# Key and query remainders spread over idle stretches and units, finer waits in three small stages, and the values of four attention blocks in one run

## The reference

```python
for layer in range(DEPTH):                                 # first block
    x = x + 0.5 * swiglu_ffn(x, ffn1_norm[layer], ...)
    if layer % 2 == 0:
        x = x + retention_dilated_mixer(x, ...)
    else:
        x = x + stick_breaking_mixer(x, ...)
    x = x + 0.5 * swiglu_ffn(x, ffn2_norm[layer], ...)
x = rms_norm(x, final_norm)
...
y_pool = pool_mixer(u, pool_w, pool_scale)                 # second block, each layer
y_nsa = nsa_mixer(q, kv[:, :, 0], kv[:, :, 1], gates, q_norm, k_norm, cmp_pe, cmp_w1, cmp_w2)
mix = jnp.concatenate([y_pool, y_nsa], axis=-1) @ w_out
x = x + gate1 * mix
h2 = rms_norm_2(x, norm2) * (1.0 + scale2) + shift2
return x + gate2 * (jnp.square(jax.nn.relu(h2 @ w_ff1)) @ w_ff2)
```

## Time and profile before

| | us |
|---|---|
| median of three runs (lowest, highest) | 3198.38 (3194.66, 3199.76) |
| the profiled execution | 3204.74 |
| its span, first to last instruction | 3203.0 |
| PE busy | 3175.9 |
| DVE busy | 1728.2 |
| POOL busy | 1303.5 |
| ACT busy | 1149.8 |
| mean granted clock of PE | 0.996 |

### The profile page before, as it was taken

How to read it: one execution, slowest core, us unless ns; L and a number is a source line. 1 busy time by engine, 2 the same in 40 slices (tenths; PEclk the granted TensorE clock), 3 DMA queues, 4 the chain that set the end, 5 groups by cost and what they waited for, 6 DMA issues and landing times.

```text
span 3203.0 us, 40631 instructions
## 1 busy us (share of the span) xinstructions
PE 3175.9 (99%) x15480; PEld 2549.3 (80%) x15480; DVE 1728.2 (54%) x2194; ACT 1149.8 (36%) x1700; POOL 1303.5 (41%) x688
## 2 busy tenths in 40 slices
PE   9999999999999999999999999999999999999999
PEld 7888886788888888887678888876888888678887
DVE  5544546554445444446764444776645556765443
ACT  4223312532223222236752222457322343753222
POOL 4777201067672777400016765030557402115600
PEclk9999999999999999999999999989999999999999
DMA  7554331155443554331124443410434342034432
GB/s 220 147 154 148 130 110 60 54 153 148 144 153 116 144 151 157 119 96 49 53 80 137 145 150 119 95 63 28 150 131 145 118 101 90 27 99 138 131 101 82
DMA packets 338612, 371.48 MB, mean 116 GB/s; under 512 B 32704, under 2 KB 287808, under 8 KB 338240
## 3 DMA queue, kind: packets, MB, share of 16 engines
q1 hardware_dynamic: 311040, 277.99, 28.1%
q0 software_dynamic: 27456, 91.94, 9.2%
HBM read 361.92 MB, written 2.18 MB: 114 GB/s over the span
## 4 chain that ended last, share of the span: by engine, by line
PE 46%; DVE 2%; ACT 2%; issue 0%; DVEq 0%; ACTq 0%
PE ps L394 19%; PE ps L779 16%; PE ps L471 2%; PE ps L685 1%; PE ps L1109 1%; PE ps L1121 1%; PE ps L1435 1%; PE ps L625 1%; PE ps L1948 1%; PE ps L566 0%; PE ps L990 0%; PE ps L1887 0%; DVE w_lo L342 0%; DVE sb_scr_lo L1412 0%; PE ps L705 0%
## 5 line engine op out<-in xcount | busy, mean ns | idle before, releaser
L338 ACT CAST w_hi<-raw 128x2048 fp32r<-128x2048 f32 x243 | 463.8, 1909 | 1139.0 <-PE ps L394 925.0
L394 PE MATMUL ps<-h_hi,w_hi 128*128 128x512 f32 x2064 | 807.3, 391 | 1.7 <-DVE w_lo L342 1.2
L394 PE MATMUL ps<-h_hi,w_lo 128*128 128x512 f32 x2064 | 804.2, 390 | 0.0
L394 PE MATMUL ps<-h_lo,w_hi 128*128 128x512 f32 x2064 | 804.1, 390 | 0.0
L342 DVE TENSOR_TENSOR w_lo<-raw,w_hi 128x2048 fp32r<-128x2048 f32 x241 | 608.5, 2525 | 248.9 <-ACT w_hi L338 248.6
L779 PE MATMUL ps<-a_hi,w_hi 128*128 128x512 f32 x1325 | 516.6, 390 | 0.4
L779 PE MATMUL ps<-a_lo,w_hi 128*128 128x512 f32 x1325 | 515.6, 389 | 0.0
L779 PE MATMUL ps<-a_hi,w_lo 128*128 128x512 f32 x1325 | 515.5, 389 | 0.0
L394 PEld LDWEIGHTS ps<-h_hi,w_hi 128*128 128x128 f32 x2064 | 388.1, 188 | 82.2 <-DVE w_lo L342 1.7
L394 PEld LDWEIGHTS ps<-h_hi,w_lo 128*128 128x128 f32 x2064 | 388.1, 188 | 81.2
L394 PEld LDWEIGHTS ps<-h_lo,w_hi 128*128 128x128 f32 x2064 | 388.2, 188 | 79.8 <-issue 0.2
(11 more groups left out here) (385 smaller groups left out, 4115.3 us busy)
## 6 DMA issues: line engine op xcount, KB each, us to landing
raw<-in_ffn_w_in SPq DMA_DIRECT2D x174, 512.0 KB, 5.0
raw<-in_w_ff SPq DMA_DIRECT2D x128, 512.0 KB, 4.3
m_in<-in_w_mod POOLq DMA_DIRECT2D x96, 512.0 KB, 4.1
raw<-in_ffn_w_out SPq DMA_DIRECT2D x88, 512.0 KB, 4.2
m_in<-in_w_ff POOLq DMA_DIRECT2D x64, 512.0 KB, 4.0
raw<-in_hyb_w_in SPq DMA_DIRECT2D x28, 512.0 KB, 4.5
raw<-in_w_in SPq DMA_DIRECT2D x28, 512.0 KB, 4.7
raw<-in_sb_w_in SPq DMA_DIRECT2D x24, 512.0 KB, 4.1
```

What stands on the lines that cost most here:

```text
L338: eng.copy(w_hi[:, e % 2], raw[:, e % 2]).then_inc(s["w_hi_done"], 1)
L394: mm = pe.matmul(ps[:, bank], wbuf[a][:, e % 2, at:at + P], hbuf[b][:, k], start=(k == 0 and n == 0), stop=(k == KC - 1 and n == 2))
```

## The change

- **Retention:** the two turns of six DVE operations are halved; three operations each stand in units 8, 9, 13 and 14.
- **Group norm:** the first mean matmul waits for three copies, the second for four, where both waited for four.
- **Stick-breaking:** chunks 4, 5 and 7 of the output projection go to banks 2, 3 and 2 instead of 7; chunks 4 and 5 wait for an exponential that was read from their bank instead of for the last eviction.
- **NSA operands:** highs and lows get orders of their own. Highs and lows of key group 0 move to steps of the key and query norm before (`nsa_pre`); the lows of queries 2 and 3 stand ahead of the compressed branch's chain, 4 and 5 behind it, 6 and 7 in units 18 and 19; the high of query 7 in unit 16. Some operands lie in other buffers.
- **Fill:** shares of a group's four units are (0, 5, 5, 6) in NSA instead of (4, 4, 4, 4), and (6, 14, 14, 14) in the dilated loop instead of (12, 12, 12, 12).
- **Values:** in the dilated loop, and in NSA from group 2 on, the values of a group's four units are done in one run in the next group's first iteration.

```diff
@@ -690,6 +690,9 @@
 
+        def om_bank(d):
+            return {4: 2, 5: 3, 7: 2}.get(d, 7)
+
@@ -697,12 +700,14 @@
             for d in range(KC):
-                if d:
-                    pe.wait_ge(s["om_x"], d)
+                if d in (4, 5):
+                    pe.wait_ge(s["sb_exp"], 2 * c.sb + 28)
+                elif d:
+                    pe.wait_ge(s["om_x"], d if d < 6 else d - 2)
...
-                        mm = pe.matmul(ps[:, 7], wbuf[a][:, c.slab % 2, at:at + P], om_part(k, b),
+                        mm = pe.matmul(ps[:, om_bank(d)], wbuf[a][:, c.slab % 2, at:at + P], om_part(k, b),
@@ -734,8 +739,17 @@
 
-            lo, per = spec["fill"]
-            return lo + (12 * d + 11) // per
+            return next(i for i in range(4 * len(spec["pairs"])) if filled(spec, i + 1) >= 12 * (d + 1))
+
+        def fill_share(spec, i):
+            return spec["fill"][i % 4] if i >= spec["from"] else 0
+
+        def filled(spec, upto):
+            return sum(fill_share(spec, i) for i in range(upto))
+
+        def in_one_run(spec, i):
+
+            return i // 4 >= spec["runs"]
@@ -951,10 +965,13 @@
 
-        def dve_turn(eng, c, xs, cos, sin, tmp, moved=m_two):
-            c.moved += 2
-            eng.wait_ge(s["rope_moved"], 32 * c.moved)
+        def dve_turn(eng, c, xs, cos, sin, tmp, moved=m_two, half=None):
+            if half != 1:
+                c.moved += 2
+                eng.wait_ge(s["rope_moved"], 32 * c.moved)
             for i, (x, _) in enumerate(xs):
+                if half is not None and i != half:
+                    continue
@@ -1078,15 +1095,27 @@
             n = 4 * len(spec["pairs"])
-            lo, per = spec["fill"]
             fill = pe_out_half(pe, c)
+
+            def values(j):
+                hp, br, I = att_unit(spec, j)
+                a, ag = c.att + j, c.attg + j // 4
+                pe.wait_ge(s["att_pt"], 2 * (a + 1))
+                if I == 3:
+                    pe.wait_ge(s["att_rc"], ag)
+                for o in range(2):
+                    mm = pe.matmul(ps[qk_rows(o), o_bank(ag), I * P:], spec["v"](br, 2 * hp + o, I),
+                                   p_T(a, o)[:, 4 * I * P:(3 * I + 4) * P], start=(I == 3), stop=(I == 0),
+                                   skip_group_check=True)
+                mm.then_inc(s["att_o"], 1)
+
...
-                if lo <= i < n:
-                    advance(fill, per)
+                if 0 <= i < n:
+                    advance(fill, fill_share(spec, i))
@@ -1099,17 +1128,11 @@
                     pe_outp_ahead(pe, c)
-                if i >= 1:
-                    hp, br, I = att_unit(spec, i - 1)
-                    a, ag = c.att + i - 1, c.attg + (i - 1) // 4
-                    pe.wait_ge(s["att_pt"], 2 * (a + 1))
-                    if I == 3:
-                        pe.wait_ge(s["att_rc"], ag)
-                    for o in range(2):
-                        mm = pe.matmul(ps[qk_rows(o), o_bank(ag), I * P:], spec["v"](br, 2 * hp + o, I),
-                                       p_T(a, o)[:, 4 * I * P:(3 * I + 4) * P], start=(I == 3), stop=(I == 0),
-                                       skip_group_check=True)
-                    mm.then_inc(s["att_o"], 1)
+                if i >= 1 and not in_one_run(spec, i - 1):
+                    values(i - 1)
+                elif i >= 1 and i % 4 == 0:
+                    for j in range(i - 4, i):
+                        values(j)
@@ -1146,7 +1169,7 @@
                     a = c.att + i
-                    eng.wait_ge(s["att_o"], a)
+                    eng.wait_ge(s["att_o"], c.att + i // 4 * 4 if in_one_run(spec, i) else a)
@@ -1376,31 +1399,38 @@
         dil_spec = {
-            "pairs": [(hp, 0) for hp in range(4)], "y": 16, "mask": "mask_dil", "gate": None, "layer": None, "fill": (8, 12), "parts": 2,
+            "pairs": [(hp, 0) for hp in range(4)], "y": 16, "mask": "mask_dil", "gate": None, "layer": None, "fill": (6, 14, 14, 14), "from": 8, "runs": 0, "parts": 2,
...
-            "pairs": [(hp, br) for hp in range(4) for br in range(2)], "y": 4, "mask": "mask_causal", "layer": 0, "fill": (7, 4), "parts": 4,
+            "pairs": [(hp, br) for hp in range(4) for br in range(2)], "y": 4, "mask": "mask_causal", "layer": 0, "fill": (0, 5, 5, 6), "from": 7, "runs": 2, "parts": 4,
...
-        QK_ORDER = (("k", 0, 0), ("q", 0), ("q", 1), ("k", 0, 1), ("q", 2), ("q", 3), ("q", 4), ("q", 5), ("q", 6),
+        HI_ORDER = (("k", 0, 0), ("k", 0, 1), ("q", 0), ("q", 1), ("q", 2), ("q", 3), ("q", 4), ("q", 5), ("q", 6),
                     ("k", 1, 0), ("k", 1, 1), ("q", 7))
-
-        def qk_count(upto):
-            return sum(2 if item[0] == "k" else 1 for item in QK_ORDER[:QK_ORDER.index(upto) + 1])
+        LO_ORDER = (("k", 0, 0), ("k", 0, 1), ("q", 0), ("q", 1), ("q", 2), ("q", 3), ("q", 4), ("q", 5),
+                    ("k", 1, 0), ("k", 1, 1), ("q", 6), ("q", 7))
+
+        def qk_count(order, upto):
+            return sum(2 if item[0] == "k" else 1 for item in order[:order.index(upto) + 1])
...
-            in_act, at = ((1, 16), (1, 19), (0, 2), (0, 3), (0, 6), (0, 7), (0, 1), (1, 14))[h]
-            return act_r[:, at] if in_act else sb_scr_lo[:, at * SEQ:(at + 1) * SEQ]
+            in_act, at = ((1, 0), (1, 1), (1, 2), (1, 3), (0, 6), (0, 7), (0, 1), (1, 14))[h]
+            return act_r[:, at] if in_act else scr_r(at)
+
+        def scr_r(at):
+            return sb_scr_lo[:, at * SEQ:(at + 1) * SEQ]
...
-            return act_r[:, (((0, 1), (2, 3)), ((12, 17), (13, 18)))[g][br][low]]
+            if (g, low) == (0, 1):
+                return scr_r(2 + br)
+            return act_r[:, ((16, 12), (19, 13), (None, 17), (None, 18))[br + 2 * low][g]]
...
@@ -1427,9 +1457,9 @@
             pe.wait_ge(s["att_max"], 2 * (c.att + i))
-            if i in (0, 4, 8, 16, 24):
-                upto = {0: ("q", 1), 4: ("k", 0, 1), 8: ("q", 3), 16: ("k", 1, 1), 24: ("q", 7)}[i]
-                pe.wait_ge(s["qk_lo"], 16 * l + qk_count(upto))
+            if i in (0, 8, 16, 24):
+                upto = {0: ("q", 1), 8: ("q", 3), 16: ("k", 1, 1), 24: ("q", 7)}[i]
+                pe.wait_ge(s["qk_lo"], 16 * l + qk_count(LO_ORDER, upto))
@@ -1710,8 +1740,8 @@
                     if step == 0:
-                        pe.wait_ge(s["ret_copy"], 4)
                         for g in (0, 1):
+                            pe.wait_ge(s["ret_copy"], 3 + g)
@@ -2242,13 +2272,11 @@
                         eng.activation(p, p, ACT.Exp, scale=HD ** -0.5).then_inc(s["cb_exp"], 1)
-                    for h in range(2, 7):
+                    for h in range(4, 7):
...
-                        eng.wait_ge(s["qk_lo"], 16 * l + qk_count(("q", 1 + 2 * br)))
+                        eng.wait_ge(s["qk_lo"], 16 * l + qk_count(LO_ORDER, ("q", 1 + 2 * br)))
                         act_k_high(eng, 1, br)
-                    eng.wait_ge(s["qk_lo"], 16 * l + qk_count(("q", 5)))
-                    act_q_high(eng, 7)
@@ -2269,6 +2297,9 @@
                             part_hi(eng, c.slab + 1, i - 8, 4)
+                        elif i == 16:
+                            eng.wait_ge(s["qk_lo"], 16 * l + qk_count(LO_ORDER, ("q", 5)))
+                            act_q_high(eng, 7)
@@ -2287,6 +2318,10 @@
                         act_hn_root(eng, c, P, 16)
+                        eng.wait_ge(s["rope_done"], 16 + 7 * l + 2)
+                        eng.wait_ge(s["cm_kp"], 2 * (l + 1))
+                        for br in range(2):
+                            act_k_high(eng, 0, br)
@@ -2307,10 +2342,8 @@
                                      k_cmp[g * HD:(g + 1) * HD, 0, 0:N_CMP]).then_inc(s["kd_copy"], 1)
-                        act_k_high(eng, 0, 0)
-                        act_q_high(eng, 0)
-                        act_q_high(eng, 1)
-                        act_k_high(eng, 0, 1)
+                        for h in range(4):
+                            act_q_high(eng, h)
@@ -2703,9 +2736,9 @@
                             gn_copy(pair - 1)
-                        if i in (8, 13):
+                        if i in (8, 9, 13, 14):
                             eng.wait_ge(s["evac_dve"], c.proj)
-                            dve_turn(eng, c, slab_rope(c, 0 if i == 8 else 1), "cos_dil", "sin_dil", nbuf)
+                            dve_turn(eng, c, slab_rope(c, i // 13), "cos_dil", "sin_dil", nbuf, half=(i - 8) % 5)
@@ -2839,7 +2872,7 @@
                             eng.wait_ge(s["om_mm"], d + 1)
-                        eng.scalar_tensor_tensor(xT[:, d], ps[:, 7], 1.0, xT[:, d], ALU.mult, ALU.add
+                        eng.scalar_tensor_tensor(xT[:, d], ps[:, om_bank(d)], 1.0, xT[:, d], ALU.mult, ALU.add
@@ -2902,7 +2935,8 @@
 
-                    dve_k_low(eng, l, 0, 1)
+                    dve_q_low(eng, l, 2)
+                    dve_q_low(eng, l, 3)
@@ -2933,8 +2967,8 @@
                                       ALU.mult).then_inc(s["cb_w"], 1)
```

(15 more changed lines are left out.)

## The result

| | before | after |
|---|---|---|
| median of seven runs (lowest, highest), us | 3198.38 (3194.66, 3203.01) | 3209.95 (3206.89, 3212.38) |
| the profiled execution, us | 3204.74 | 3206.89 |
| its span, us | 3203.0 | 3205.1 |
| TensorE busy, us | 3175.9 | 3164.1 |
| mean granted clock | 0.996 | 0.998 |

The ratio is 1.0031, with a 95% interval of 1.0021 to 1.0041: slower by some 10 us. The forecast was 3202 with a range of 3184 to 3212; the time lies in the range, but beyond the 0.2% that the forecast called no change. A few executions of the kernels took from 3636 to 12593 us instead of some 3200, and the ratios leave them out.

What follows compares the result with a forecast made beforehand. TensorE, busy 3175.9 of 3203.0 us, was taken as the bound, so only its gaps and small stream losses could be won. Gains 21.4 less losses 25.2 made 3.8 us slower than the median 3198.38: 3202, range 3184 to 3212.

Steps and rivals of the forecast that it cites:

- Small stages: Retention, group norm and stick-breaking: shorter TensorE waits gain 0.9, 0.9 and 1.6 us.
- Start of NSA: Both NSA layers: TensorE gaps ahead of L1887 go, 6.5 us; layer 0's clock no longer falls, 2.2 (bounds 0 and 2.9).
- a difference of a few us carries over unscaled: Whole kernel: sums made on the profiled 3204.74 us apply to the median 3198.38, 0.2% below.
- Moved work: NSA remainders and casts moved into VectorE and ScalarE gaps: nothing lost; L1004 0.5 us late in layer 1, with slack.
- Values in a run, NSA, and reciprocals: NSA units: skips gain 7.0 and copy waits 1.7 us; reciprocals lose 13.5 and 0.9, exponentials 2.4 and 1.6.
- The waits for reciprocals: NSA units 12, 16, 20, 24, 28, two layers: TensorE stalls 1.35 us at L1095, together 13.5.
- The waits for exponentials: Filled NSA groups: TensorE arrives 0.2 us early in each of 12, 2.4 lost; layer ends lose 1.6.
- The price of a skip: NSA: each skipped switch from scores to values and back saves about 0.19 us, 36 times: 7.0.
- The four waits for evictions: Dilated units 11, 12, 14, 15: chunks wait for their bank's eviction, 0.9, 2.3, 1.1 and 2.2 us.
- for reciprocals at units 4 and 8: Dilated stage: waits for reciprocals at these units lose 0.3 us, part of the 6.8.
- 0.6 gained: Dilated loop: 12 skipped switches to values save 0.05 us each, by the transposes alone.
- The rival: NSA: new gaps of 1.35 us every 13 us make the clock fall, four falls giving 3214 us; chance 0.12.

Runs made afterwards that it cites:

- small_only: Kernel before with only halved turns, the group norm's wait and the stick-breaking banks changed: 3196.74 us, ratio 0.9996.
- operands_only: Changed kernel with both fills even and no values in runs, leaving the operands' order and the small stages: 3191.86 us, ratio 0.9979.
- both_even: Changed kernel with the NSA and dilated fills both even again, values still in runs: 3195.50 us, ratio 0.9991.
- three_ahead: Changed kernel with the dilated stage as before and, in NSA, three of a group's four values ahead of the wait for reciprocals: 3189.52 us, ratio 0.9971.
- no_runs: Changed kernel with each unit's values behind the next unit's scores again, in NSA and dilated stage, fills still uneven: 3199.05 us, ratio 1.0003.
- dil_even: Changed kernel with the dilated fill even again, (12, 12, 12, 12), all else as changed: 3200.48 us, ratio 1.0005.
- evac_first: Changed kernel with NSA fill even and without runs; in the dilated stage VectorE evicts a finished chunk ahead of weight remainder L360: 3196.60 us, ratio 0.9999.
- late_rec: Changed kernel with the reciprocals' four transposes moved behind the next unit's scores on TensorE, in both attention loops: 3205.49 us, ratio 1.0019.

## Why the prediction was right in its mechanisms and low in its size, point by point

**The size of the whole.** It had +3.8 us, measured are +10 (0.31%). The sign was right, the bound of "no change" was not. The largest part of the difference is the dilated stage, which lost 10.5 where 6.8 less 0.6 was said: 3.2 of that is the clock, most of the rest waits for exponentials. Another 1.6 is moved work that was put at nothing.

**Small stages, 3.4 predicted.** Retention gave 1.4 (0.9 taken), group norm 0.9, stick-breaking 1.4; 0.4 was given back ahead of the dilated stage (0.4 to 0.8 in the other kernels), where TensorE now comes before work it used to find done (L1036 waits 0.21 and 0.40 in after, by row). Predicted: 3.4; in the trace of after: 3.3; by small_only's ratio 1.3, with an interval from 4.2 gained to 1.6 lost.

**Start of NSA, 6.5 and 2.2 predicted.** L1917 (the old L1887) follows the scores at once and takes 3.60 for its eight matmuls in layer 0:

```profile
2134.95 0.40 PE L1465 MATMUL ps<-sb_scr_lo,act_r 128*128 128x512 f32 x1
2135.19 3.60 PE L1917 MATMUL ps<-scr,v_cmp 128*128 128x512 f32 x8
```

The gaps of 3.2 and 3.3 are gone as said. The 2.2 for the clock was right for this profiled execution (6.2 gained, 3.2 of it the gap) and may be too much for the median, since the slow stretch was shorter in the one other profile of this code. Here the step that failed is "a difference of a few us carries over unscaled": the profile of before stood 6.4 us above its median, and what made it so was in part this very term.

**Moved work, nothing predicted.** This term was wrong. VectorE's four remainders (L1453) put L1021, the old L1004 of the earlier trace rows, 2.9 us later in layer 1, at 2687.20, of which 1.5 is the shift of everything there: 1.4 late, where 0.5 was said, on a chain that was taken to have slack. The chain ends with L1029, and TensorE waits for it:

```profile
2684.44 2.83 DVE L1453 TENSOR_TENSOR sb_scr_lo<-act,act_r 64x512 fp32r<-64x512 f32 x4
...
2689.91 1.09 PE L1036 MATMUL ps<-consts,act 128*128 128x128 f32 x8 [0.59 <-DVE act L1029]
```

The same wait of 0.59 stands at 2099.49 in layer 0; from start to start each costs 0.8, together 1.6. The kernel before and small_only have no such wait; of the eleven kernels with the moved remainders seven have it in layer 0 and four in layer 1. Six of them (not after) also wait 0.39 to 0.56 by row in layer 0 for L2968, the end of the compressed branch's chain on VectorE; why it is late in those was not followed up. The table's borders leave both out.

**Values in a run, NSA, and reciprocals.** Predicted for the two layers: 7.0 + 1.7 gained; 13.5 + 0.9 + 2.4 + 1.6 lost; net 9.7 lost. Measured: 9.0 lost. That the net came out is in part luck, since two terms were too small and offset each other.

The waits for reciprocals are 1.40 from the earliest possible start where 1.35 was said, ten times: 14.0. The waits for exponentials, said to be 0.2 in each of 12 groups, are 0.07 by row but 0.23 from the earliest start in ten of them, and 0.91 (0.74 by row, where ScalarE has casts ahead of them) in one group of each layer: 4.1 us instead of 2.4.

The price of a skip was said to be 0.19 and is 0.29, between the starts in the steady groups of operands_only and after: the last score takes 0.09 more ahead of values than ahead of transposes (0.32 against 0.23 with 512 columns), the two pairs of values take 0.05 and 0.10 more than a pair inside a run (0.37 and 0.42 against 0.32 with 384 columns), and the first transpose behind values takes 0.165 instead of 0.109. The prediction had compared the last pair with the first, which stands behind a switch too. For 36 skips this is 10.4 us instead of 7.0.

With these prices the steady group of operands_only (12.19 us, in which nothing waits) gives the others: three skips and the waits of after, counted from the earliest start, give 13.04 (measured 13.01); those of both_even 12.51 (12.55); two skips and the one wait of three_ahead 11.89 (11.85). So a run saves 0.9 us a group, and in the changed kernel uncovers more than that.

**Dilated stage, 6.8 predicted less 0.6.** The four waits for evictions were predicted as 0.9, 2.3, 1.1 and 2.2; from the earliest possible start they are 0.9, 2.4, 1.15 and 2.05 (the rows above are 0.16 to 0.24 less each). This is the step that held best. The term that failed is the 0.3 "for reciprocals at units 4 and 8": what came instead are waits for the exponentials in the units before the fill, 0.61 and 0.72 by row, and 0.29 for L2167, a copy of ScalarE that the fill needs. They come from the run (no_runs has none over 0.17 there): the values had covered them, and the "0.6 gained" is, with these waits, 0.7 lost in dil_even and both_even, beside operands_only. The second miss there is the clock.

**The clock.** The rival placed it in NSA, behind gaps of 1.35 us, where it did not happen: not one stretch at 1.2 GHz lies in the NSA units of any of these kernels. It happened in the dilated stage, behind the gaps of 2.16 and 1.89, and cost some 1.6 us each time (from 605.47 on, in the fence of the dilated stage, a matmul's row has 0.63 instead of 0.39, and the starts are 0.43 apart instead of 0.23, for five matmuls and the four transposes behind them; from 625.63 on for seven matmuls). In all four kernels with the uneven dilated fill and runs the clock fell at 605; in the three of them with L360 ahead of the eviction it fell at 625 as well; in the other kernels with this stage profiled it fell at neither. That evac_first lost the fall at 625 together with the wait speaks for the wait as the cause there. The length of one gap does not decide it alone: 1.37 did not do it, nor did 3.14 in the earlier trace rows and 3.30 at the same place of small_only, while 3.05 in the earlier trace rows and 2.39 in small_only's layer 0 were followed by a fall. And each of the thirteen profiles has a fall at 2063 to 2091 or at 2648 to 2674 with no gap over 0.5 us ahead of it (in after a granted clock of 0.64 over 2068 to 2072, with TensorE busy all of it). Why it falls there stays open.
The Trainium skill, "TensorE: Matmul & The Clock Gate", section "A second HAM failure mode: psum-queue depth-cycling", had been read as speaking for a fall behind frequent short gaps. Five gaps of 1.24 us in each layer, one every 13 us, did not bring one, so the trace does not bear out that reading for this spacing.

**Sum.** From the trace of after: small stages -3.3, start of NSA -6.2 and -3.4, moved work +1.6, dilated +10.5 (3.2 of it the clock), NSA units +9.0. Together +8.2, or up to 3 more where an execution of the kernel before has no slow stretch at the start of NSA. By the ratio it is +9.9, from +6.7 to +13.1; the medians differ by 11.6.

## What to carry to other kernels

Moving filler away from a place is costed by what is then awaited there, counted from the start of the chain that releases it, and not from the filler's own length. What a wait or a switch costs is read from start to start: the idle time of a row left out 0.16 to 0.24 us of each wait here, and waits of 0.15 us showed in no row at all. And only work that does not hang on the same chain can cover that wait, as late_rec and three_ahead show. When chunks of a double-buffered product no longer end where the other engine's turn ends, each chunk waits for an eviction queued behind a whole unit's work. Two edits that share a cover (the runs and the fill) should be tried together and apart: both lost here, while runs and the uneven fill with older values ahead of the wait took 0.34 us less a steady group than neither.

## What the runs showed of the hardware

A gap of 2.16 us on TensorE in the dilated stage was followed by a stretch at 1.2 GHz in four profiled executions of four, at the same place, and one of 1.89 in three of three; gaps of 1.24 to 1.37 us in the attention stages were not, nor were those of 3.14 and 3.30 at the start of NSA in layer 1. In layer 0 those of 3.05 (before) and 2.39 (small_only) were. The clock also fell where TensorE had no gap over 0.5 us (after, 2068 to 2072).

Going from scores to values and on to transposes costs 0.29 us beside going from scores straight to transposes, which costs nothing (0.23 us from the last score to the next start, as between scores). The first of several transposes takes 0.165 us to the next start behind values (three_ahead) and behind a wait (after), and 0.109 behind fill matmuls or scores that end in time (operands_only, late_rec).
